# Routing by one table of pairwise comparisons, another order around the last tile, and block 2's list read first

## The chip, the cores and the metric

The kernel runs on one core of a Trainium2 chip. Each time is the device time of one execution in microseconds (us). The engines named below are PE (TensorE, the matrix multiplier), DVE (VectorE), ACT (ScalarE), POOL (GpSimd) and SP (SyncE, which here only starts DMAs). They run their own instruction streams and meet at semaphores.

## The reference

One step of a one-layer encoder over 1024 prompt frames and 32 sample frames, width 1024. First a mixer (an mLSTM with four heads and a multi-scale pooling), then a mixture of 16 experts in 4 groups of 4:

```python
x = x + mix @ w_out
x = x + hier_moe(rmsnorm(x, norm2_g), w_rg, b_rg, w_re, b_re, w_gate, w_up, w_down)

def hier_moe(x, ...):
    pg = softmax(x @ w_rg + b_rg)                 # 4 groups
    pg_top, g_idx = top_k(pg, 1)
    le = (x @ w_re + b_re) of the group chosen    # 4 experts
    pv, pi = top_k(softmax(le), 2)
    pv = pv / sum(pv)
    y = sum over the 2 experts e: pg_top * pv_e * ((silu(x @ w_gate[e]) * (x @ w_up[e])) @ w_down[e])
```

`top_k` takes the lower index where two values are equal.

## The kernel before

**Tiles.** The 1056 rows are nine tiles (`NT` = 9, `LAST` = 8) of 128 rows, the sample frames being a tile of 32. In a round `i` of a loop over the tiles every engine does its part of tile `i` (projections), tile `i-1` (mLSTM, pooling, `w_out`) and tile `i-2` (router). Each engine's order is the order in which the code is written. The block `if i == NT` is round 9: the rest of the last tile and the router of tile 7 (`LAST - 1`), without projections to fill PE. Round 10 holds the router of tile 8.

**Router of a tile.** PE transposes the tile (`h2_transposes`), DVE scales it into `h2T` (`h2_evac`, L1016), PE multiplies by the router weights (`router`), DVE copies (`partial_logits`, `lgT`, L1056), PE sums (`router_sums`), DVE adds the bias (`logits`, L1062). `routing` then finds the group and two experts in three calls of `first_max` (L1068 to L1072), 24 small DVE instructions that each wait for the one before. It writes one-hot rows `oh[:, t, 0..2, :]`, the third being the sum (L1096). PE counts with it (`ranks`), and DVE (`places`, L1136 to L1144) turns the counts into a slot for each row in its expert's list. POOL writes the entries into the lists in HBM (`scatter`, L541).

**Experts.** After the tiles come 16 blocks of at most 150 rows of one expert (150 rows in blocks 1 and 2, then six of 130, two of 135, two of 140, and 150 again). For a block POOL reads its list (`load_ids`, L557), gathers its rows from HBM in 5 indirect DMAs (L551), DVE transposes them (`gather_turn`, L1407) and scales them (`gather_scale`, L1413), PE does gate and up (`gate_up`, L1527) and down, ACT and DVE the silu and the product (`products`, L1428), DVE turns the results back (`results`, L1436) and weighs them (`gate_rows`, L1443), and POOL adds them into `z_d` in 5 indirect DMAs (L599). `results` of block j waits until the additions of block j-1 have landed. SP loads an expert's weights (3 MB) when PE has freed the former ones. Block 1 is put together early: the rows of tiles 0 to 6 that belong to it are gathered (`first`, turned by `first_turn`, L1115), those of tiles 7 and 8 are picked by a matmul with a 0/1 matrix (`first_picks`, DVE L1109), and `first_rows` (L1129) sums both.

**POOL behind the tiles.** After `scatter(8)` POOL reads the list of block 1 (start of expert 0's list), copies it (L639), reads the list of block 2, gathers block 2, and then waits for the table of blocks, which DVE computes meanwhile, to read the list of block 3. Small instructions on `pad` (`stand`, `carry_wait`, L595, L499) stand between them.

## Time and profile before

| | us |
|---|---|
| median of 3 runs | 939.91 (939.53 to 940.20) |
| span of the profiled execution, first to last instruction | 939.7 |
| PE busy | 880.8 (94% of the span) |
| DVE busy | 431.1 (46%) |
| POOL busy | 374.6 (40%) |
| ACT busy | 154.5 (16%) |

The profiled execution was recorded with its span alone; nothing is recorded of what lies around it. The median of the other runs is 0.2 us more than this span. Times in rows are from the start of the span. A busy share is a mean over stages with different limits: what an edit is worth is read where it stands. L numbers are lines of the kernel before. "bank" is PSUM; `win` and `wout` name SBUF areas that the expert stage uses again for its own buffers, and `h_d` in the rows is the HBM copy of the normed rows.

### The profile page before, as it was taken

The page shows a single profiled execution, that of the slowest core. Times are in us where ns is not written, and L with a number is a line of the kernel's source. Part 1 is how long each engine was busy: PE and PEld are TensorE (multiplying, and loading weights), DVE is VectorE, ACT ScalarE, POOL GpSimd, SP SyncE. Part 2 cuts the span into 40 slices and gives each one's busy share as a digit, 9 for nine tenths or more (in the row PEclk, how much of TensorE's full clock was granted, in tenths as well). Part 3 has the DMA queues.
Part 4 walks back from the last instruction along what each step waited for, and adds up shares of the span by engine and source line. Part 5 has one row for each costly group of instructions (what it writes and reads, how often), then busy time and mean ns, then how long its engine had stood idle before and what let it go on. Part 6 is the DMA issues. An engine that isn't in the chain of part 4 may idle for free.

```text
span 939.7 us, 16689 instructions
## 1 busy us (share of the span) xinstructions
PE 880.8 (94%) x6339; PEld 755.1 (80%) x6339; DVE 431.1 (46%) x1166; ACT 154.5 (16%) x456; POOL 374.6 (40%) x576
## 2 busy tenths in 40 slices
PE   5989999999999999999989799999999999999960
PEld 3974987869588695886945699999999999999920
DVE  3144474645646456463557843333333333333264
ACT  2031212121311213111131210000000000000071
POOL 4040031210302103021150258767767776777524
PEclk9989999999999999999999899999999999999985
DMA  9930203030110301003027389999999999999883
GB/s 328 280 151 1 68 1 80 12 79 1 28 52 1 79 1 34 25 1 57 1 62 291 71 294 299 327 352 335 360 346 333 327 322 326 315 319 314 248 305 115
DMA packets 90039, 163.15 MB, mean 174 GB/s; under 512 B 48887, under 2 KB 59027, under 8 KB 81770
## 3 DMA queue, kind: packets, MB, share of 16 engines
q1 hardware_dynamic: 70062, 136.43, 41.5%
q0 software_dynamic: 17728, 25.28, 11.2%
q8 instruction: 41, 0.67, 0.3%
q10 hardware_dynamic: 2188, 0.59, 0.3%
q14 instruction: 20, 0.16, 0.0%
HBM read 139.83 MB, written 25.87 MB: 176 GB/s over the span
## 4 chain that ended last, share of the span: by engine, by line
PE 51%; DMA 16%; issue 11%; POOL 11%; DVE 9%; ACT 1%; POOLq 1%; DVEq 0%; SPq 0%; ACTq 0%
PE bank L1527 48%; DMA z_d<-wout,win 12%; POOL z_d L599 7%; DVE wout L1443 2%; POOL wout L551 2%; PE bank L1532 1%; DVE wout L1436 1%; DVE win L1482 1%; DMA wout<-h_d,idt 1%; DMA h2T<-z_d 1%; DVE win L1407 1%; PE bank L1732 0%; DMA xbuf<-in_x_prompt 0%; POOL pad L595 0%; PE bank L1645 0%
## 5 line engine op out<-in xcount | busy, mean ns | idle before, releaser
L1527 PE MATMUL bank<-wout,win 128*128 128x150 f32 (+3 forms) x2048 | 246.3, 282 | 1.1 <-DVE wout L1129 1.1
L1527 PEld LDWEIGHTS bank<-wout,win 128*128 128x128 f32 x2048 | 244.7, 190 | 1.2 <-DVE wout L1129 1.2
L1527 PE MATMUL bank<-hT,win 128*128 128x128 f32 (+1 forms) x1536 | 182.9, 279 | 0.0
L1527 PEld LDWEIGHTS bank<-hT,win 128*128 128x128 f32 x1536 | 178.6, 192 | 1.5 <-issue 1.2
L1527 PE MATMUL bank<-win 128*128 128x130 f32 (+5 forms) x1024 | 137.3, 294 | 2.7 <-DVE win L1428 1.4
L599 POOL DMA_INDIRECT z_d<-wout,win x75 | 125.2, 1669 | 27.1 <-issue 26.8
L1527 PEld LDWEIGHTS bank<-win 128*128 128x128 f32 (+2 forms) x1024 | 125.5, 191 | 12.3 <-issue 10.3
L1527 PE MATMUL bank<-win,hT 128*128 128x260 f32 (+3 forms) x512 | 122.2, 417 | 3.0 <-DVE xbuf L1247 1.5
L1527 PE MATMUL bank<-wout,mixT 128*128 128x512 f32 (+1 forms) x384 | 116.8, 487 | 1.8 <-ACT mixT L845 1.7
L1527 PEld LDWEIGHTS bank<-win,hT 128*128 128x128 f32 (+1 forms) x512 | 77.1, 173 | 43.0 <-issue 34.1
L1436 DVE STREAM_TRANSPOSE wout<-bank 128x480 f32<-128x480 f32 (+1 forms) x45 | 25.1, 603 | 156.7 <-DMA z_d<-wout,win 155.2
L1527 PEld LDWEIGHTS bank<-wout,mixT 128*128 128x128 f32 (+1 forms) x384 | 50.8, 163 | 57.1 <-issue 54.4
L534 POOL TENSOR_SCALAR_AFFINE_SELECT dexp<-dexp 128x512 f32<-128x512 f32 (+1 forms) x9 | 5.4, 596 | 200.2 <-DVE dexp L1051 200.2
L551 POOL DMA_INDIRECT wout<-h_d,idt x75 | 73.8, 984 | 20.8 <-issue 20.5
L927 ACT ACTIVATE win<-bank 128x150 f32<-128x150 f32 (+3 forms) x64 | 18.1, 287 | 330.9 <-PE bank L1527 308.7
L512 POOL COPY ulast<-ubuf 128x60 f32<-128x60 f32 x7 | 3.9, 555 | 119.5 <-ACT ubuf L824 119.4
L1407 DVE STREAM_TRANSPOSE win<-wout 128x1280 f32<-128x1280 f32 x15 | 37.8, 2517 | 13.0 <-DMA wout<-h_d,idt 13.0
L1428 DVE TENSOR_TENSOR win<-bank,win 128x150 f32<-128x150 f32 (+3 forms) x64 | 17.7, 293 | 50.6 <-ACT win L927 50.6
L541 POOL DMA_INDIRECT ids_d<-ent,slots x18 | 18.4, 1021 | 49.2 <-DVE slots L1144 44.7
L595 POOL TENSOR_TENSOR pad<-pad 1x1 f32<-1x1 f32 x61 | 18.3, 301 | 26.0 <-DMA z_d<-wout,win 13.3
L1034 DVE RECIPROCAL sig<-sig 128x512 f32<-128x512 f32 x8 | 26.8, 3352 | 0.3
L1443 DVE TENSOR_TENSOR wout<-wout,win 128x1280 f32<-128x1280 f32 x15 | 22.5, 1497 | 7.4 <-POOL win L610 5.8
(308 smaller groups left out, 812.0 us busy)
## 6 DMA issues: line engine op xcount, KB each, us to landing
win<-in_w_gate SPq DMA_DIRECT2D x32, 1024.0 KB, 6.3
win<-in_w_up SPq DMA_DIRECT2D x32, 1024.0 KB, 9.2
win<-in_w_down SPq DMA_DIRECT2D x32, 1024.0 KB, 10.6
win<-in_w_in SPq DMA_DIRECT2D x4, 2048.0 KB, 20.1
xbuf<-in_x_prompt SPq DMA_DIRECT2D x8, 512.0 KB, 3.8
wout<-in_w_out SPq DMA_DIRECT2D x1, 4096.0 KB, 15.6
z_d<-xbuf SPq DMA_DIRECT2D x32, 128.0 KB
h_d<-xn SPq DMA_DIRECT2D x8, 512.0 KB, 2.7
```

Of the source, the lines that this page charges most:

```text
L541: g.indirect_dma_start(out=ids_d, out_offset=bass.IndirectOffsetOnAxis(ap=slots[0:R, n, t:t + 1].bitcast(U32), axis=0), in_=ent[0:R, n, t, ...
L551: g.indirect_dma_start(out=dst[:, c, :], out_offset=None, in_=h2_q, in_offset=bass.IndirectOffsetOnAxis(ap=idt[:, c:c + 1].bitcast(U32), a ...
L595: g.tensor_tensor(pad[:, c:c + 1], pad[:, 0:1], pad[:, 0:1], ALU.mult)
L599: g.indirect_dma_start(out=z_q, out_offset=bass.IndirectOffsetOnAxis(ap=idp[:, c:c + 1].bitcast(U32), axis=0), in_=yrow[:, c, :], in_offse ...
L927: a.activation(sgl[:, f % 2, 0:n], B[GB[f]][:, 0:n], ACT.Silu).then_inc(silu_ready, 1)
L1034: link(v.reciprocal(sig[0:R, b, :], sig[0:R, b, :]))
L1407: v.transpose(xgS.rearrange("p k a i -> p a k i"), xg.rearrange("p a (i k) -> p a k i", k=KD)).then_inc(xt_raw, 1)
L1428: v.tensor_tensor(hid[:, f, 0:n], B[GB[f]][:, n:2 * n], sgl[:, f % 2, 0:n], ALU.mult).then_inc(hid_ready, 1)
L1436: v.transpose(yrow[:, :, 32 * m0:32 * m1].rearrange("p a (m i) -> p m a i", i=32), y_window(b, m1 - m0, r)).then_inc(y_ready, 1)
L1443: v.tensor_tensor(yrow, yrow, ents[3][:, :, 1:2].broadcast_to([P, NP, PIECE]), ALU.mult).then_inc(y_gated, 1)
L1482: out = v.scalar_tensor_tensor(out=dq, in0=sq, scalar=fs[0:R, 3, c:c + 1], in1=wq, op0=ALU.mult, op1=ALU.mult)
L1527: return nc.tensor.matmul(out, lhsT, rhs, start=first, stop=last)
```

## The change

- `routing` compares all pairs of four values at once, for the group logits and the four groups of expert logits together (a 5 x 4 x 4 table `duel`), and sums it both ways to give each value its rank. The group is the one with the highest rank, the two experts those with the two highest. After 8 instructions `oh[:, t, 2, :]` is written and PE may count. The rest is split into `picks_of` (3 instructions), `gaps` (5) and `shares` (3). In rounds 2 to 8 they stand one behind the other where `routing` stood.
- Round 9 on DVE is in another order: `mix_start` of tile 8 (without its last instruction, now `decayed`) stands ahead of `norm_x1` of tile 7; `new_state` and `partial_logits(7)` stand behind the instruction that ACT waits for; `first_turn` is split into 2, 2 and 1 pieces. On ACT the copy `xp` of tile 7 (L855) stands behind the decay matrix of tile 8.
- The router of tile 8 stands in round 9, its slots (`seats`) behind `first_rows`; `seats(7)` behind `places(8)`; the scaling of the normed tile 8 (`scale_x1`) behind `gaps(8)`.
- On PE the state transposes stand behind `ranks(8)`, and the first half of tile 8's transposes need no longer wait for the second half of its residual.
- POOL reads block 2's list and gathers its rows first, then reads block 1's list, then block 3's.

```diff
@@ POOL
+            load_ids(CAP)
+            fetch_block(2, 1, 2)
             load_ids(0)
-            pool.wait_ge(ids_in, 32)
-            g.tensor_copy(ents[0], idraw).then_inc(carried, 1)
-            pool.wait_ge(carried, 2)
-            load_ids(CAP)
-            g.tensor_copy(ents[1], ents[0]).then_inc(rolled, 1)
-            pool.wait_ge(rolled, 1)
-            fetch_block(2, 2)
             after(pool, "table_ready", 1)
...
+            pool.wait_ge(ids_in, 48)
+            stand(4)
+            g.tensor_copy(ents[2], idraw).then_inc(rolled, 2)
+            pool.wait_ge(rolled, 2)
+            pool.wait_ge(carried, 4)
+            g.tensor_copy(ents[1], ents[0]).then_inc(carried, 2)
+            pool.wait_ge(carried, 6)
             load_ids(pool.value_load(tabi[0:1, NB + 3:NB + 4], min_val=0, max_val=NE * CAP))
-            pool.wait_ge(carried, 5)
-            g.tensor_copy(ents[2], ents[1]).then_inc(rolled, 1)
-            pool.wait_ge(rolled, 2)
-            g.tensor_copy(ents[1], ents[0]).then_inc(carried, 1)
-            pool.wait_ge(carried, 6)
             fetch_block(3, 6)
@@ ACT, round 9
                     decay_matrix(LAST)
+                    picked_rows(LAST - 1)
                     head_norm(LAST)
                     mix_a(LAST)
                     route_exps(LAST - 1)
                     norm_2(LAST)
+                    picked_rows(LAST)
@@ DVE
+                link(v.tensor_tensor(ge, five.unsqueeze(3).broadcast_to(cubed), five.unsqueeze(2).broadcast_to(cubed), ALU.is_ge))
+                link(v.tensor_tensor(ge, ge, below[0:R].unsqueeze(1).broadcast_to(cubed), ALU.mult))
+                link(v.tensor_reduce(out=ahead, in_=ge, axis=AX.X, op=ALU.add))
+                link(v.tensor_reduce(out=lost, in_=ge.rearrange("p g a b -> p g b a"), axis=AX.X, op=ALU.add))
+                link(v.tensor_tensor(rank, lost, ahead, ALU.subtract))
+                link(v.tensor_tensor(goh, rank[:, 0], seat[0:R, 0], ALU.is_equal))
+                two = cube_of(R)
+                link(v.tensor_tensor(two, rank[:, 1:], seat[0:R, 1].unsqueeze(1).broadcast_to([R, EG, EPG]), ALU.is_le))
+                v.tensor_tensor(oh[0:R, t, 2, :].rearrange("p (g e) -> p g e", e=EPG), two, wide(goh, [R, EG, EPG]), ALU.mult
+                                ).then_inc(S["route_ready"], 1)
@@ DVE, round 9
                     mix_start(LAST)
+                    norm_x1(LAST - 1)
+                    decayed(LAST)
                     mix_b(LAST)
                     h2_evac(LAST - 1)
-                    first_turn()
+                    first_turn(range(0, 2))
                     numerators(LAST)
-                    partial_logits(LAST - 1)
                     head_out(LAST)
                     logits(LAST - 1)
                     routing(LAST - 1)
+                    picks_of(LAST - 1)
+                    gaps(LAST - 1)
+                    first_turn(range(4, NP))
                     first_scale()
+                    shares(LAST - 1)
                     residual(LAST)
                     places(LAST - 1)
                     h2_evac(LAST)
-                    norm_x1(LAST)
-                    continue
+                    dve.wait_ge(pick_ready, 1)
+                    rms_x1(LAST)
+                    partial_logits(LAST)
+                    logits(LAST)
+                    routing(LAST)
+                    picks_of(LAST)
+                    places(LAST)
+                    seats(LAST - 1)
+                    gaps(LAST)
+                    scale_x1(LAST)
+                    first_rows()
+                    shares(LAST)
+                    seats(LAST)
+                    break
@@ DVE, in head_out
+                if t == LAST:
+                    new_state(LAST)
+                    partial_logits(LAST - 1)
+                    first_turn(range(2, 4))
                 after(dve, "hs0", t + 1)
@@ PE, round 10
                     first_picks(LAST - 1)
-                    state_transposes()
                 if 2 <= i:
                     ranks(i - 2)
                 if i == NT + 1:
+                    state_transposes()
                     first_picks(LAST)
```

The instructions of DVE and POOL in their order, at the three places that matter (a time is not in these rows).

**Place 1: DVE in round 9, from the norm of tile 7 to `h2_evac(7)`.** `sm` is the rms of tile 7 and `xn` its normed rows; PE's pooling matmul waits for `dcy`; `dexp` is the decay matrix. Before:

```order
L1259 TENSOR_SCALAR xn<-xbuf,sm 128x1024
L1041 COPY hmt<-bank 128x128
L1043 COPY dcy<-bank 128x4
L1046 TENSOR_TENSOR kw<-bank,hmt 128x512
L1051 TENSOR_TENSOR dexp<-bank,dexp 128x512
L1236 TENSOR_TENSOR mixT<-bank,psc 128x512
L1016 TENSOR_TENSOR h2T<-bank,g 128x512 x2
```

Now:

```order
L1048 COPY hmt<-bank 128x128
L1050 COPY dcy<-bank 128x4
L1053 TENSOR_TENSOR kw<-bank,hmt 128x512
L993 TENSOR_SCALAR sm<-sm 128x1
L994 TENSOR_TENSOR sm<-sm 128x1
L995 TENSOR_TENSOR sm<-sm 128x1
L996 TENSOR_SCALAR sm<-sm 128x1
L997 TENSOR_TENSOR sm<-sm 128x1
L1306 TENSOR_SCALAR xn<-xbuf,sm 128x1024
L1063 TENSOR_TENSOR dexp<-bank,dexp 128x512
L1276 TENSOR_TENSOR mixT<-bank,psc 128x512
L1023 TENSOR_TENSOR h2T<-bank,g 128x512 x2
```

The three instructions on `hmt`, `dcy` and `kw` moved ahead of the norm of tile 7; `dexp` stayed behind it.

**Place 2: DVE behind `places(8)`.** The first two rows are the pick of tile 8, `slotf` and `slots` the list places, the `wout` row is `first_rows`, `kw<-cnt` the start of the table. Before:

```order
L1107 SCALAR_TENSOR_TENSOR rt<-oh,rt 128x1
L1109 TENSOR_SCALAR win<-place_of,rt,sm 128x150
L1142 TENSOR_TENSOR rt<-oh,rt 128x16
L1143 TENSOR_REDUCE slotf<-rt 128x1
L1142 TENSOR_TENSOR rt<-oh,rt 128x16
L1143 TENSOR_REDUCE slotf<-rt 128x1
L1144 CAST slots<-slotf 128x2
L1129 SCALAR_TENSOR_TENSOR wout<-bank,g2m,win 128x5x30 x8
L1359 SCALAR_TENSOR_TENSOR kw<-cnt,iof 128x16
```

Now, behind the pick of tile 8 (`kept` holds the places of tile 7):

```order
L1174 TENSOR_TENSOR rt<-oh,kept 128x16
L1175 TENSOR_REDUCE slotf<-rt 128x1
L1174 TENSOR_TENSOR rt<-oh,kept 128x16
L1175 TENSOR_REDUCE slotf<-rt 128x1
L1176 CAST slots<-slotf 128x2
L1115 TENSOR_REDUCE rt<-rt 128x1
L1116 TENSOR_TENSOR rt<-rt 128x4
L1117 TENSOR_TENSOR rt<-oh 128x16
L1118 TENSOR_TENSOR rt<-rt 128x16
L1119 TENSOR_REDUCE rt<-rt 128x1
L1306 TENSOR_SCALAR xn<-xbuf,sm 128x1024
L1154 SCALAR_TENSOR_TENSOR wout<-bank,g2m,win 128x5x30 x8
```

and behind `first_rows`:

```order
L1124 SCALAR_TENSOR_TENSOR rt<-rt 128x1
L1126 RECIPROCAL ent<-rt 128x1
L1127 TENSOR_TENSOR ent<-ent,rt 128x1
L1174 TENSOR_TENSOR rt<-oh,rt 128x16
L1175 TENSOR_REDUCE slotf<-rt 128x1
L1174 TENSOR_TENSOR rt<-oh,rt 128x16
L1175 TENSOR_REDUCE slotf<-rt 128x1
L1176 CAST slots<-slotf 128x2
L1429 SCALAR_TENSOR_TENSOR kw<-cnt,iof 128x16
```

Between the pick of tile 8 and `first_rows` stand 11 instructions instead of 5, and tile 8's own slots stand behind `first_rows`, ahead of the table.

**Place 3: POOL behind the last scatter.** `idraw` receives a list, the `wout` rows are the 5 gathers of a block. Before:

```order
L557 DMA idraw<-ids_d 128x1x10 [waits h2_stored,out_done,scat1,scat0]
L639 COPY win<-idraw 128x10 [waits ids_in]
L557 DMA idraw<-ids_d 128x1x10 [waits carried]
L642 COPY win<-win 128x10
L595 TENSOR_TENSOR pad<-pad 1x1 [waits xt_raw,ids_in,rolled]
L562 TENSOR_SCALAR idt<-idraw,qf 128x5
L564 COPY win<-idraw 128x10
L499 TENSOR_TENSOR pad<-pad 1x1 [waits carried]
L551 DMA wout<-h_d,idt 128x256 x5
L646 TENSOR_LOAD tabi [waits table_ready]
L646 ISA x2
```

Now:

```order
L564 DMA idraw<-ids_d 128x1x10 [waits h2_stored,out_done,scat1,scat0]
L602 TENSOR_TENSOR pad<-pad 1x1 [waits xt_raw,ids_in]
L569 TENSOR_SCALAR idt<-idraw,qf 128x5
L571 COPY win<-idraw 128x10
L506 TENSOR_TENSOR pad<-pad 1x1 [waits carried]
L558 DMA wout<-h_d,idt 128x256 x5
L564 DMA idraw<-ids_d 128x1x10
L648 TENSOR_LOAD tabi [waits table_ready]
L648 ISA x2
```

and from there to block 3's list:

```order
L602 TENSOR_TENSOR pad<-pad 1x1 [waits ids_in]
L657 COPY win<-idraw 128x10
L660 COPY win<-win 128x10 [waits carried,rolled]
L662 TENSOR_LOAD tabi [waits carried]
L662 ISA x2
L564 ISA
L564 DMA idraw<-ids_d 128x1x10
L602 TENSOR_TENSOR pad<-pad 1x1 [waits xt_raw,ids_in]
L569 TENSOR_SCALAR idt<-idraw,qf 128x5
```

One list load instead of two stands ahead of block 2's gathers, and behind them block 1's list is awaited before block 3's is asked for.

## Rows read from the trace of the kernel before

**Rows 1.** The page: span, then each engine's busy time, share of the span, instructions.

```profile
span 939.7 us, 16689 instructions
...
PE 880.8 (94%) x6339; PEld 755.1 (80%) x6339; DVE 431.1 (46%) x1166; ACT 154.5 (16%) x456; POOL 374.6 (40%) x576
```

**Rows 2.** Timeline, PE, 461 to 551: start, busy us, work [idle before <- releaser].

```profile
461.92 0.29 PE L1527 MATMUL bank<-oh,ustrict 128*128 128x16 f32 x2
...
493.07 1.13 PE L1527 MATMUL bank<-dlt,poolw 128*128 128x128 f32 x8 [2.69 <-DVE dcy L1043]
...
508.35 0.66 PE L1732 MATMUL bank<-ident,isb 128*128 128x128 f32 x4 [1.18 <-DVE isb L1209]
...
520.67 0.65 PE L1527 MATMUL bank<-h2T,wr 128*32 128x128 f32 x16 [1.97 <-DVE h2T L1016]
...
522.93 4.35 PE L1527 MATMUL bank<-win 128*128 128x150 f32 x16
...
534.27 16.59 PE L1527 MATMUL bank<-wout,win 128*128 128x150 f32 x128 [1.15 <-DVE wout L1129]
```

**Rows 3.** Waits of PE, 560 to 900: us in total, times, longest.

```profile
PE bank L1527 <- DVE win L1428: 1.4, 3, 0.7
```

**Rows 4.** Timeline, DVE, results of blocks 3, 10, 11, 14 and 15.

```profile
608.06 1.65 DVE L1436 STREAM_TRANSPOSE wout<-bank 128x480 f32<-128x480 f32 x3 [8.16 <-DMA z_d<-wout,win]
...
766.34 1.65 DVE L1436 STREAM_TRANSPOSE wout<-bank 128x480 f32<-128x480 f32 x3 [14.33 <-DMA z_d<-wout,win]
...
789.60 1.64 DVE L1436 STREAM_TRANSPOSE wout<-bank 128x480 f32<-128x480 f32 x3 [14.70 <-DMA z_d<-wout,win]
...
856.67 1.65 DVE L1436 STREAM_TRANSPOSE wout<-bank 128x480 f32<-128x480 f32 x3 [9.50 <-DMA z_d<-wout,win]
...
875.49 0.68 DVE L1436 STREAM_TRANSPOSE wout<-bank 128x480 f32<-128x480 f32 x1 [3.81 <-DMA z_d<-wout,win]
```

**Rows 5.** Timeline, DVE, 452 to 538.

```profile
452.60 0.15 DVE L1068 TENSOR_REDUCE rt<-rt 128x1 f32<-128x4 f32 x1
...
457.16 0.18 DVE L1096 TENSOR_TENSOR oh<-oh 128x16 f32<-128x16 f32 x1
...
492.57 0.28 DVE L1041 COPY hmt<-bank 128x128 f32<-128x128 f32 x1
...
531.31 0.17 DVE L1144 CAST slots<-slotf 128x2 int32<-128x2 f32 x1
531.88 2.34 DVE L1129 SCALAR_TENSOR_TENSOR wout<-bank,g2m,win 128x150 f32<-128x150 f32 x8 [0.40 <-PE bank L1527]
...
537.28 0.29 DVE L1370 TENSOR_TENSOR kw<-kw,rt 128x128 f32<-128x128 f32 x1
```

**Rows 6.** Timeline, ACT, at 490.8.

```profile
490.81 2.04 ACT L855 ACTIVATE win<-xbuf 128x1024 f32<-128x1024 f32 x1
```

**Rows 7.** Window 522 to 523: us, PE busy, granted clock, DMA share, GB/s.

```profile
522.00:523.00 1.00, 0.51 (x3) 0.50 0.01 1
```

**Rows 8.** Timeline, POOL, 532 to 559.

```profile
532.28 0.96 POOL L541 DMA_INDIRECT ids_d<-ent,slots  x1 [9.93 <-DVE slots L1144]
...
536.76 0.76 POOL L557 DMA_DIRECT2D idraw<-ids_d  x1 [2.24 <-issue]
...
539.53 0.70 POOL L557 DMA_DIRECT2D idraw<-ids_d  x1 [0.30 <-POOL win L639]
...
549.09 0.79 POOL L557 DMA_DIRECT2D idraw<-ids_d  x1
...
555.93 1.39 POOL L595 TENSOR_TENSOR pad<-pad 1x1 f32<-1x1 f32 x1 [5.59 <-DVE win L1407]
...
558.19 1.09 POOL L551 DMA_INDIRECT wout<-h_d,idt  x1 [0.17 <-issue]
```

**Rows 9.** DMA issues of 549 to 550: KB each, median us to landing.

```profile
idraw<-ids_d POOLq DMA_DIRECT2D x1, 5.0 KB, 4.3
```

**Rows 10.** The same for 536 to 537.5.

```profile
idraw<-ids_d POOLq DMA_DIRECT2D x1, 5.0 KB, 2.2
```

More of the change, by code:

```diff
@@ L1098, in routing, with shares @@
+            def shares(t):
+                R = ROWS[t]
                 after(dve, "rexp", t + 1)
@@ L1319, in _ @@
                     routing(i - 2)
+                    picks_of(i - 2)
+                    gaps(i - 2)
+                    shares(i - 2)
                     places(i - 2)
```

114 lines of the change are left out of this document (69 added, 45 removed).

## The prediction

> **What bounds the kernel now.** I read the page first. PE is busy for 94% of the span and DVE, POOL and ACT for less than half of it [rows 1], so an edit on DVE pays only where PE, or what decides the end, waits for it. PE's timeline shows where that is. In the tile rounds PE comes to `ranks` at 461.92 without a wait, and DVE had the one-hot rows ready at 457.34; the waits stand behind 488, in rounds 9 and 10: 2.69 us for `dcy`, 1.18 for the heads, 1.97 for `h2T`, 1.15 for `first_rows` [rows 2, 5]. At 522 to 523 the granted clock is 0.50, the 1.2 GHz level, after two thirds of the time since 517.6 stood idle, and `first_picks(7)` takes 4.35 us there, twice the 2.2 that it takes at 2.4 GHz [rows 2, 7].
>
> Then the expert stage. PE looks full, but it waits three times for DVE's products, 1.4 us in all [rows 3]. DVE's `results` waits in every block for the landing of the block before (8.16, 14.33, 14.70, 9.50 us) [rows 4]. These landings form a second chain: landed additions, results, weighing, 5 scatter issues on POOL, landing. Between blocks 3 and 14 it takes (856.67 - 608.06)/11 = 22.6 us a block [rows 4]. PE takes less for the 130-row blocks and more for the 150-row blocks: the chain falls behind, stops PE where PE waits for products, and gets level again at block 15, where `results` waits 3.81 us for the landing and then still for PE. So the end moves by what the chain moves; what PE alone gains at its start is lost again in the three waits. I follow both.
>
> **The change part by part.**
>
> *Routing in the seven tile rounds.* 24 dependent instructions take 457.34 - 452.60 = 4.74 us [rows 5]. No trace shows the 80-wide compare. 16 elements cost 0.18 and 128 elements 0.29 [rows 5]; these are the bounds, and I take 0.24 from the line between them. Four such and four of about 0.17, with 0.035 between two, give 1.9 us up to `route_ready` (1.7 with the small price for all, 2.1 with the large one). In these rounds PE comes 4.6 us later than the result, so the cover is wide and I take 0 for them; the instructions put behind it (11, some 2.1 us) keep the sum below the old one.
>
> *Round 9, first half.* `dcy` is copied right after the residual. DVE copies `hmt` at 492.57 now [rows 5], behind ACT's three instructions and the norm; it can at 489.1, so PE starts pooling at 490.3 instead of 493.07. The next wait is for the decay product: ACT starts it behind a copy of 2.04 us that began at 490.81 [rows 6]; without it DVE's product ends 1.0 us earlier than before, POOL's mask follows, and PE idles 0.9 us. Since the long idle stretch goes, I let PE keep 2.4 GHz there. I get the router of tile 7 at 496.0 against 499.3: 3.3 us. `head_out` then no longer stands behind `new_state` and `lgT` (four and one instructions, 1.05 us): the heads reach PE at 504.0 instead of 508.35, 4.35 us earlier. This holds through `w_out`, since DVE's longer list there ends at 510.7 and the second half of the residual comes at 512.5.
>
> *Round 9, second half.* `seats(7)`, five instructions of 0.2 with their gap, leaves the way: 0.95. The scaling of the normed tile leaves it: 0.75. So the logits of tile 8 come 6.05 us earlier, 6.3 if the clock holds; the routing gives 2.8 less than 4.7: `route_ready` at 518.95 instead of 527.8. `first_picks(7)` ends then too if it runs at 2.4 GHz. Counts and state transposes change places, the pick of tile 8 is ready at 520.65, 9.9 us earlier. But DVE now does 11 instructions (0.95 + 0.95 + 0.75 us) ahead of `first_rows`: that starts at 523.25 instead of 531.88 and PE begins block 1 at 525.6 instead of 534.27 [rows 2, 5], 8.65 us earlier. This is PE's lead, not yet the end's.
>
> *Slots of tile 8.* They are cast at 531.31 (ready 531.48) [rows 5], ahead of `first_rows`. Now `first_rows` (2.34), `shares` (0.55) and `seats` (0.95) come first: 527.1, only 4.4 us earlier. Queued behind them on DVE is the table; it ends near 537, and its readers come later than that. On POOL everything waits for these slots.
>
> *POOL's list loads.* From the first list load to the second it is 539.53 - 536.76 = 2.77 us [rows 8]. This trip leaves the way to block 2's gathers: 4.4 + 2.8 = 7.2 us, so the last gather, which ended at 549.09, ends at 541.9. What is late next is block 3. Before, its list was asked for at 549.09 and lay ready when `stand` could go at 555.93 [rows 8]. Now block 1's list goes first: asked for at 541.9, landed 4.3 later [rows 9] at 546.2, two copies with their gaps 0.9, a register load and the issue about 1.0; then block 3's own load, asked for at 548.1. Its landing is bounded by 2.2 (quiet queue) [rows 10] and 4.3 [rows 9]; I take the middle, since the gathers are gone from the queue but weights are under way. So the list is in at 551.3, while DVE turned block 2 at 548.6 already: a new wait of 2.7 us. `stand`, 1.39 us long beside DVE's scaling [rows 8], should fall behind it and be short; 1.1 us later the gathers of block 3 begin, 552.4 instead of 558.19 [rows 8]. The chain starts 5.8 us earlier. Ends: 2.2 and 0.4 for load and issue give 7.4; both trips at 4.3 and a long `stand` give 3.5.
>
> The Trainium skill, "DMA: Bandwidth & Descriptors", section on the anatomy of one DMA, gives a fixed cost of about 2.0 us to such a small load, whatever it stands behind. Rows 9 and 10 differ by twice with the same 5 KB. By that rule both trips would cost 2.0, the list would lie there when block 2 is turned, and the sum would be about 1.5 us lower; the row of 4.3, from this very place, decides.
>
> *What the lead does to the chain.* PE's lead over the chain grows by 8.65 - 5.8 = 2.85 us. The late blocks, where the lag is large, have longer steps (block 10 to 11: 789.60 - 766.34 = 23.26 [rows 4]). If the first three or four steps take 0.3 more each for the earlier lag, 1.0 us is lost. Bounds: 0, and 0.66 in each of 12 steps (below).
>
> Sum: 939.7 - 5.8 + 1.0 = 934.9 for this execution; its span is 0.2 under the median, so 935.1.
>
> **The rivals.**
>
> *The clock still falls in round 10.* For: PE still idles 1.5 and 0.5 us around 514 to 516.5, and it fell after such idling before [rows 7]. Against: half of that idling is gone. Then `first_picks(7)` costs 4.35, not 2.2, counts and pick come 2 us later, and slots and chain with them: 937.0.
>
> *PE leads, the chain follows.* If the landings are long only because the DMA engines are behind, an earlier start of the weights moves them too, or block 3's list comes in unnoticed. Then the end moves 8.3 us: 931.6. Against: `results` waits for landings in every block already.
>
> *Nothing reaches the end.* The lists take the long end (3.5), the clock falls (2.0) and the chain gives 1.0 back: 939.4.
>
> *Slower, by the chain's step.* One mechanism: with the weights of each block asked for earlier against the scatters, landings take longer in every step, not only the first. At the longest step seen, 23.26 against 22.6, 12 steps cost 7.9 us: 939.9 - 5.8 + 7.9 = 942.0. It decides from 0.48 us a step on. For: the long steps are those with the largest lag. Against: late steps with large lag were as often normal, and PE's waits would cap the lag as they do now.
>
> **How the numbers follow.** 935.1 has 0.45, the clock 0.25, PE's lead 0.15, nothing 0.09, slower 0.06. The likeliest case alone reaches from 933.5 to 937.5. The range that leaves out 2 in 10 takes in PE's lead and the clock case with its long trips: 931.3 to 938.6. A measurement here tells 0.2%, 1.9 us, from no change. Under 938.0 lie the first and third cases and nearly all of the clock case: 0.84; within 0.2%: 0.10; slower: 0.06.
>
> **What will show it.** Right: pooling of tile 8 on PE without a wait near 490.3; heads at 504; PE's first expert matmul at 525 to 526 and the last `slots` cast near 527; gathers of block 2 beginning near 535.8; a wait of POOL for block 3's list of 2 to 3 us, and its gathers near 552; PE's waits for products growing from 1.4 to about 4 us; `results(3)` near 602. Wrong: a clock of 0.50 around 518 (then 937), block 3's gathers before 550 (then under 934), steps over 23 us on average (then no gain), or a PE that shows no more waits than before while the end still moves by over 8 us.

## The result, and the profile after

The changed kernel takes 942.77 us (median of 14 runs, 940.44 to 945.47), the kernel before 940.07 (14 runs): ratio 1.0033, 95% interval 1.0023 to 1.0043. It is slower by a third of a per cent; the forecast was 935.1. Timed once more it gave 1.0026 (1.0016 to 1.0037). The two profiled executions of the changed kernel have spans of 939.8 and 940.6, the two of before 939.7 and 936.7; a span is 1.6 to 2.0 below its run's time. Both profiles of the change are needed, since they lose the gain in two places. Left out of the rows and ratios below are one run of e3, 2601.6 us long, and one of the kernel before, 1880.1 us.

The page of the first (the same parts as in [rows 1]):

```profile
span 939.8 us, 16630 instructions
...
PE 876.3 (93%) x6339; PEld 751.2 (80%) x6339; DVE 427.0 (45%) x1106; ACT 154.6 (16%) x456; POOL 371.5 (40%) x575
```

PE's timeline, first profile of the change (columns as in [rows 2]; L1597 answers to L1527 there):

```profile
488.23 1.06 PE L1597 MATMUL bank<-dlt,poolw 128*128 128x128 f32 x8
...
519.42 2.28 PE L1597 MATMUL bank<-win 128*128 128x150 f32 x16 [0.21 <-DVE win L1134]
...
523.89 2.31 PE L1597 MATMUL bank<-wout,win 128*128 128x150 f32 x16 [1.15 <-DVE wout L1154]
...
557.05 18.39 PE L1597 MATMUL bank<-wout,win 128*128 128x150 f32 x128 [8.39 <-DVE wout L1483]
...
583.47 14.45 PE L1597 MATMUL bank<-wout,win 128*128 128x130 f32 x128
```

Rounds 9 and 10 went as forecast: no wait for `dcy`, and PE starts the experts at 523.89, in the second profile at 524.38, where it started at 534.27 [rows 2] and in the second profile of before at 532.57. Then it waits 8.39 us ahead of block 2, and block 3 starts at 583.47, with the kernel before at 583.39. The second profile loses it elsewhere, a part ahead of block 2 and 5.28 us inside it:

```profile
524.38 1.95 PE L1597 MATMUL bank<-wout,win 128*128 128x150 f32 x11 [1.15 <-DVE wout L1154]
...
552.45 16.59 PE L1597 MATMUL bank<-wout,win 128*128 128x150 f32 x128 [1.62 <-DVE wout L1483]
574.31 11.33 PE L1597 MATMUL bank<-win 128*128 128x150 f32 x64 [5.28 <-issue]
585.48 6.75 PE L1597 MATMUL bank<-wout,win 128*128 128x130 f32 x59
```

In both profiles PE waits for nothing from block 3 to the last block, so the gain is gone when block 3 starts. The reason stands on POOL. First profile (answers to [rows 8]; L548 scatters list entries, L564 loads a list, L558 gathers rows; the small `pad` at L602 starts when the list is in):

```profile
522.01 0.98 POOL L548 DMA_INDIRECT ids_d<-ent,slots  x1 [0.30 <-issue]
528.84 0.97 POOL L548 DMA_INDIRECT ids_d<-ent,slots  x1 [5.84 <-DMA ids_d<-ent,slots]
...
533.09 0.77 POOL L564 DMA_DIRECT2D idraw<-ids_d  x1 [2.01 <-issue]
540.05 0.18 POOL L602 TENSOR_TENSOR pad<-pad 1x1 f32<-1x1 f32 x1 [6.19 <-DMA idraw<-ids_d]
...
541.14 1.11 POOL L558 DMA_INDIRECT wout<-h_d,idt  x1 [0.17 <-issue]
...
547.27 0.78 POOL L564 DMA_DIRECT2D idraw<-ids_d  x1
553.80 0.18 POOL L602 TENSOR_TENSOR pad<-pad 1x1 f32<-1x1 f32 x1 [5.75 <-DMA idraw<-ids_d]
...
555.71 0.70 POOL L564 DMA_DIRECT2D idraw<-ids_d  x1 [1.27 <-DVE win L1477]
557.98 0.18 POOL L602 TENSOR_TENSOR pad<-pad 1x1 f32<-1x1 f32 x1 [1.57 <-DMA idraw<-ids_d]
...
559.04 1.11 POOL L558 DMA_INDIRECT wout<-h_d,idt  x1 [0.18 <-issue]
```

The second profile of the change, the same stretch:

```profile
533.72 0.77 POOL L564 DMA_DIRECT2D idraw<-ids_d  x1 [2.11 <-issue]
536.00 0.18 POOL L602 TENSOR_TENSOR pad<-pad 1x1 f32<-1x1 f32 x1 [1.52 <-DMA idraw<-ids_d]
...
543.20 0.78 POOL L564 DMA_DIRECT2D idraw<-ids_d  x1
549.90 0.18 POOL L602 TENSOR_TENSOR pad<-pad 1x1 f32<-1x1 f32 x1 [5.92 <-DMA idraw<-ids_d]
...
551.80 0.70 POOL L564 DMA_DIRECT2D idraw<-ids_d  x1 [1.27 <-DVE win L1477]
558.22 0.18 POOL L602 TENSOR_TENSOR pad<-pad 1x1 f32<-1x1 f32 x1 [5.71 <-DMA idraw<-ids_d]
...
559.28 1.11 POOL L558 DMA_INDIRECT wout<-h_d,idt  x1 [0.18 <-issue]
```

Read the pairs of load and `pad`: the same 5 KB take 7.0, 6.5 and 2.3 us in the first profile and 2.3, 6.7 and 6.4 in the second. Together the three take 15.8 and 15.4 us, and block 3's rows are asked for at 559.04 and 559.28, behind the 558.19 of [rows 8], where the forecast had 552.4.

What stands beside them is SP's queue of the first profile, block 2's weights (with the kernel before, the first of them is issued at 542.79):

```profile
532.41 0.35 SPq L380 DMA_DIRECT2D win<-in_w_gate  x1
532.80 0.43 SPq L380 DMA_DIRECT2D win<-in_w_up  x1
540.51 0.33 SPq L380 DMA_DIRECT2D win<-in_w_gate  x1
540.88 0.44 SPq L380 DMA_DIRECT2D win<-in_w_up  x1
544.60 4.47 SPq L386 DMA_DIRECT2D win<-in_w_down  x2
```

and the windows (us, busy time of each engine, clock, DMA share, GB/s), first before, then the change:

```profile
533.00:540.00 7.00, 5.85 (x48) 5.76 (x47) 6.35 (x23) 0.00 (x0) 2.63 (x5) 1.00 0.07 8
```

```profile
533.00:540.00 7.00, 7.00 (x57) 7.00 (x56) 2.57 (x12) 2.06 (x4) 0.77 (x1) 1.00 0.89 303
547.00:554.00 7.00, 1.67 (x14) 1.44 (x12) 1.01 (x1) 0.00 (x0) 1.24 (x4) 1.00 1.01 371
556.00:558.00 2.00, 0.95 (x4) 0.95 (x5) 2.00 (x3) 0.00 (x0) 0.43 (x2) 0.50 0.09 3
```

A list takes 7.0 and 6.5 us where the DMA share is 0.89 and 1.01, and 2.3 us where it is 0.09; before it found 0.07. SP asks for block 2's weights when PE is through the first half of block 1's gate and up, 8.5 us behind PE's start of block 1 both before (534.27, 542.79) and in the first profile (523.89, 532.41), so PE's gain brought them here.

In the second profile SP asks 10.2 us behind that start, since PE's granted clock fell to 0.50, the 1.2 GHz level, in the middle of it. That profile's first weights, and the window 526 to 528 of the first and the second profile:

```profile
534.58 0.35 SPq L380 DMA_DIRECT2D win<-in_w_gate  x1
526.00:528.00 2.00, 2.00 (x18) 2.00 (x17) 1.83 (x6) 0.00 (x0) 0.00 (x0) 1.00 0.12 26
526.00:528.00 2.00, 2.00 (x10) 2.00 (x9) 1.77 (x6) 0.00 (x0) 0.00 (x0) 0.50 0.31 75
```

Block 1 takes PE 26.4 us there, without its wait, and 24.8 in the first profile. With the 8.5 us of the first profile the weights would have been asked for at 532.9 (an estimate), 0.8 us ahead of the list at 533.72: by this estimate it is the slower clock that let this list through, at a price of 1.7 us in block 1.

Inside block 2 of the second profile, DVE explains the wait that has no named releaser on PE:

```profile
566.52 1.55 DVE L1513 TENSOR_TENSOR wout<-wout,win 128x1280 f32<-128x1280 f32 x1 [12.58 <-POOL win L617]
571.32 2.48 DVE L1477 STREAM_TRANSPOSE win<-wout 128x1280 f32<-128x1280 f32 x1 [3.24 <-DMA wout<-h_d,idt]
573.72 0.49 DVE L1498 TENSOR_TENSOR win<-bank,win 128x150 f32<-128x150 f32 x2
```

Block 2's products (573.72), which PE needs, stand behind the turn of block 3's rows, and these have landed only at 571.3.

### The profile page after: what moved, and what is told of

The parts are those of the page before. It is cut to its first block and busy times, and to the rows that moved or that the text cites. A ratio compares the mean times of both kernels' runs of the same rounds, so it can differ in the third digit from the quotient of the medians.

```text
span 939.8 us, 16630 instructions
## 1 busy us (share of the span) xinstructions
PE 876.3 (93%) x6339; PEld 751.2 (80%) x6339; DVE 427.0 (45%) x1106; ACT 154.6 (16%) x456; POOL 371.5 (40%) x575
## 5 line engine op out<-in xcount | busy, mean ns | idle before, releaser
L1597 PE MATMUL bank<-wout,win 128*128 128x150 f32 (+3 forms) x2048 | 248.2, 283 | 9.5 <-DVE wout L1483 8.4
L1597 PEld LDWEIGHTS bank<-wout,win 128*128 128x128 f32 x2048 | 246.5, 191 | 9.8 <-DVE wout L1483 8.6
L1597 PE MATMUL bank<-hT,win 128*128 128x128 f32 (+1 forms) x1536 | 182.9, 279 | 0.0
L1597 PEld LDWEIGHTS bank<-hT,win 128*128 128x128 f32 x1536 | 178.6, 192 | 1.5 <-issue 1.2
L1597 PE MATMUL bank<-win 128*128 128x130 f32 (+5 forms) x1024 | 135.0, 291 | 0.3 <-DVE win L1134 0.2
L1597 PEld LDWEIGHTS bank<-win 128*128 128x128 f32 (+2 forms) x1024 | 123.5, 188 | 9.8 <-issue 9.4
L1597 PE MATMUL bank<-win,hT 128*128 128x260 f32 (+3 forms) x512 | 121.1, 415 | 3.3 <-DMA win<-in_w_in 1.8
L1597 PE MATMUL bank<-wout,mixT 128*128 128x512 f32 (+1 forms) x384 | 116.8, 487 | 1.7 <-ACT mixT L849 1.7
L1597 PEld LDWEIGHTS bank<-win,hT 128*128 128x128 f32 (+1 forms) x512 | 76.5, 172 | 42.7 <-issue 33.5
L1597 PEld LDWEIGHTS bank<-wout,mixT 128*128 128x128 f32 (+1 forms) x384 | 50.8, 163 | 57.1 <-issue 54.4
L558 POOL DMA_INDIRECT wout<-h_d,idt x75 | 74.6, 994 | 20.8 <-issue 20.8
L548 POOL DMA_INDIRECT ids_d<-ent,slots x18 | 18.3, 1018 | 49.5 <-DVE slots L1176 39.2
L602 POOL TENSOR_TENSOR pad<-pad 1x1 f32<-1x1 f32 x62 | 17.9, 289 | 27.7 <-DMA idraw<-ids_d 13.5
```

The lines of the kernel that those rows point to most:

```text
L548: g.indirect_dma_start(out=ids_d, out_offset=bass.IndirectOffsetOnAxis(ap=slots[0:R, n, t:t + 1].bitcast(U32), axis=0), in_=ent[0:R, n, t, ...
L558: g.indirect_dma_start(out=dst[:, c, :], out_offset=None, in_=h2_q, in_offset=bass.IndirectOffsetOnAxis(ap=idt[:, c:c + 1].bitcast(U32), a ...
L602: g.tensor_tensor(pad[:, c:c + 1], pad[:, 0:1], pad[:, 0:1], ALU.mult)
L1597: return nc.tensor.matmul(out, lhsT, rhs, start=first, stop=last)
```

## The experiments

Five rounds each, ratio to the kernel before run beside it on the same chip; each group of runs (e, f, g, h, i) had another chip. "Rows 3" is POOL's first gather for block 3, "PE 3" PE's start of block 3, "last" the end of PE's last expert work, all of one profile (us).

| kernel | rows 3 | PE 3 | last | span | median | ratio (95%) |
|---|---|---|---|---|---|---|
| before | 558.19 | 583.39 | 908.15 | 939.7 | 940.1 | |
| before, again | 556.51 | 581.69 | 904.29 | 936.7 | 939.6 | 0.9994 (0.9983, 1.0006) |
| changed | 559.04 | 583.47 | 906.48 | 939.8 | 942.8 | 1.0033 (1.0023, 1.0043) |
| changed, again | 559.28 | 585.48 | 908.08 | 940.6 | 942.3 | 1.0026 (1.0016, 1.0037) |
| e1 weights after list | 559.05 | 583.02 | 906.79 | 938.7 | 940.4 | 1.0009 (0.9993, 1.0025) |
| e2 changed, old lists | 561.00 | 587.78 | 910.38 | 943.9 | 946.5 | 1.0072 (1.0057, 1.0087) |
| e3 before, new lists | 560.79 | 582.72 | 908.81 | 941.0 | 941.8 | 1.0024 (1.0008, 1.0040) |
| e4 scatters together | 553.25 | 576.19 | 899.59 | 931.8 | 936.5 | 0.9959 (0.9943, 0.9974) |
| f1 own list buffer | 560.26 | 586.79 | 909.76 | 944.4 | 945.4 | 1.0018 (0.9985, 1.0050) |
| f2 e3 and own buffer | 556.53 | 583.27 | 906.49 | 940.9 | 941.2 | 1.0008 (0.9998, 1.0019) |
| f3 both mends | 548.95 | 574.06 | 896.67 | 931.9 | 932.8 | 0.9912 (0.9892, 0.9932) |
| f3, again | 549.13 | 574.43 | 898.01 | 933.4 | 934.8 | 0.9953 (0.9936, 0.9969) |
| f7 weights after rows | 548.85 | 575.85 | 898.45 | 933.7 | 934.5 | 0.9930 (0.9909, 0.9950) |
| g1 routing alone | 557.29 | 582.64 | 905.25 | 938.0 | 939.7 | 0.9998 (0.9988, 1.0008) |
| g2 no ACT stores | 554.39 | 579.16 | 901.76 | 934.0 | 938.8 | 0.9996 (0.9978, 1.0014) |
| h1 products first | 558.77 | 584.76 | 908.68 | 942.3 | 943.7 | 1.0045 (1.0028, 1.0063) |
| h3 f3, slots first | 550.98 | 577.51 | 900.11 | 934.6 | 936.2 | 0.9964 (0.9952, 0.9977) |
| h5 f3, products first | 549.66 | 574.89 | 897.49 | 932.8 | 934.0 | 0.9949 (0.9931, 0.9967) |
| i1 e1, products first | 559.56 | 581.43 | 906.74 | 939.0 | 941.1 | 1.0014 (0.9997, 1.0031) |
| i2 e1, again | 560.21 | 583.30 | 906.87 | 939.3 | 940.8 | 1.0009 (0.9992, 1.0025) |

Over all twenty profiles "last" comes 346.3 to 350.0 us behind "rows 3" and 322.6 to 326.1 behind "PE 3"; in nine of them PE runs the last stretch in 322.6 without a wait. The ratio isn't that of the medians: f1 has two of its twelve runs near 934.7, and its ratio is 1.0018 where the medians alone would give 1.0054.

**e1, block 2's weights after its list.** In the changed kernel:

```
+                sp.wait_ge(ids_in, 32)
                 load_gate_up(1, half)
```

> The changed kernel, with block 2's gate and up weights asked for on SP only once block 2's list has landed. Theory (the list's load collides with these weights: it is asked for at 533.09, 0.7 us after them, and takes 6 to 7 us where it took 2.2): the list lands in 2.2 to 3 us, the first gather of block 2 is issued near 536.5 instead of 541.14, gathers of block 3 near 554 instead of 559.04, PE's wait ahead of block 2 shrinks from 8.4 to about 4 us, and the end is 4 to 5 us under the changed kernel (about 938.3, ratio to before 0.998). Rival (the list is slow whatever the weights do, POOL being late through its scatters alone): landing stays at 6 us or more, the weights only come later, end the same as the changed kernel or 1 to 3 us over it.

The list lands in 2.3 us and the first gather is issued at 537.29: the weights made it slow. But block 1's list, asked for at 543.40 between the weights of 542.97 and 546.61, takes 6.9 us, and block 3's, asked for at 552.22, 5.8. Block 3's rows are no earlier than in the changed kernel. The theory is right on the collision and wrong on its worth: it only moves to the next list. The time did fall by about 2 us against the changed kernel, here and in i2 (1.0009 twice, against 1.0033 and 1.0026), where 4 to 5 had been expected; rows 3, PE 3 and "last" don't show where these 2 us come from.

**e2 and e3, the order of the lists by itself.** e2 puts POOL's old sequence (block 1's list, copy, block 2's list, gathers, block 3's list) into the changed kernel, e3 the new one (`load_ids(CAP)`, `fetch_block(2, 1, 2)`, `load_ids(0)`, copies, block 3's list) into the kernel before.

> The changed kernel with POOL's lists in the order of before (block 1's list first, then block 2's), all else as changed. Theory (the new order is worth its trip, the collision is the fault): two trips of which the first takes 6 to 7 us; block 2's first gather near 545 instead of 541.1, the end 1 to 4 us over the changed kernel (944 to 947). Rival (the new order is the fault, since block 1's list now stands in the way of block 3's): gathers of block 3 come at or before 558, the end under the changed kernel by 1 to 3 us.

> The kernel before with POOL's lists alone in the new order. Theory (without PE's lead the weights of block 2 are asked for at 542.8, behind the list's landing): landing 2.2, block 2's first gather near 540.2 instead of 542.96, gathers of block 3 1 to 2.5 us earlier than 558.19, end 1 to 2.5 us under before (937.6 to 939). Rival (the order is the fault): block 3's list comes late, its gathers at or behind 558.2, the end the same as before or up to 3 us over it.

e2: as the theory, 4 us over the changed kernel; PE waits 9.2 us ahead of block 2. e3: the rival. POOL in e3:

```profile
539.98 1.11 POOL L551 DMA_INDIRECT wout<-h_d,idt  x1 [0.18 <-issue]
...
546.09 0.79 POOL L557 DMA_DIRECT2D idraw<-ids_d  x1
551.73 0.18 POOL L595 TENSOR_TENSOR pad<-pad 1x1 f32<-1x1 f32 x1 [4.85 <-DMA idraw<-ids_d]
...
553.63 0.70 POOL L557 DMA_DIRECT2D idraw<-ids_d  x1 [1.27 <-issue]
559.73 0.18 POOL L595 TENSOR_TENSOR pad<-pad 1x1 f32<-1x1 f32 x1 [5.40 <-DMA idraw<-ids_d]
...
560.79 1.11 POOL L551 DMA_INDIRECT wout<-h_d,idt  x1 [0.18 <-issue]
```

Block 2's gathers come 3.0 us earlier than before (542.96), block 3's 2.6 later than in [rows 8]: two lists one behind the other now stand between them, 5.6 and 6.1 us, where block 3's alone was asked for at 549.09 and was hidden. The order saves a trip where it doesn't count and puts one where it does, without any lead of PE.

**e4, g2, the scatters.** e4: POOL issues tile 8's entries without waiting for tile 7's.

```
+                if t == LAST - 1:
+                    return
                 for name in ("scat0", "scat1"):
                     after(pool, name, 16 * (t + 1))
```

g2 leaves out ACT's eight stores of the recurrent state, normalisers and pooling history, so it doesn't return these outputs.

> The changed kernel, in which POOL doesn't wait for the landing of tile 7's scattered list entries before it issues tile 8's (it waits for both behind them). Theory (collision): scatters of tile 8 at 525.4 instead of 528.84, the list asked for near 530, ahead of the weights at 532.4, and landed in 2.2 to 3 us; block 2's first gather near 534 instead of 541.1; the end 5 us or more under the changed kernel (936 to 938.5). Rival (the landing of a list is slow for another reason, not by what is asked beside it): the list is asked for 3.3 us earlier and still takes 6 us or more, gathers near 538, end 2 to 3 us under the changed kernel.

> The changed kernel without ACT's eight stores of the recurrent state, normaliser, pooling history (these outputs are left out), which are issued from 520.98 to 525.8. Theory S (POOL's scatter of tile 7's entries, issued at 520.5 and 522.0, takes 5.8 us to land since these stores, in lines of a few bytes, stand in the queues beside it): landing in 2 to 2.5 us, tile 8's scatter at 525.5 instead of 528.84, the list asked for near 529.5, ahead of the weights at 532.4, and the end as with the scatters together, 5 to 7 us under the changed kernel (936 to 938). Rival (it's SP's 512 KB store of the normed rows at 521.62, which stays): scatter of tile 8 at 528 to 529 as before, end the same as the changed kernel.

e4 does what the theory says: scatter at 526.91, list asked for at 531.46, ahead of the weights (533.72), in after 2.3 us, block 3's rows at 553.25, 5.8 us ahead of the changed kernel. g2: the wait for tile 7's entries falls from 5.8 to 3.7 us, not to 2. SP's 512 KB store stays and may be the rest; no run takes it away. In its profile the list then lands in 2.3 us and block 3's rows are asked for at 554.39. Its runs spread from 935.6 to 945.1; the ratio lies under that of the changed kernel (0.9996 against 1.0026, intervals apart) and shows no gain over before. That the stores share in the hold-up is shown; its worth is read better from e4, which leaves nothing out.

**f1, f2, f3, a tile of its own for block 1's list,** so that block 3's is asked for straight behind the gathers; f3 adds e4 and asks for block 1's right behind block 2's:

```
             load_ids(CAP)
+            load_ids(0, idone, idone_in)
             fetch_block(2, 1)
...
+            load_ids(pool.value_load(tabi[0:1, NB + 3:NB + 4], ...))
+            pool.wait_ge(idone_in, 16)
+            g.tensor_copy(ents[2], idone).then_inc(rolled, 2)
```

> The changed kernel, with block 1's list landing in a tile and on a semaphore of its own, so that block 3's list is asked for right behind block 2's gathers instead of behind block 1's list and two copies. Theory A (block 3's list stands on the chain: block 1's list takes 6 to 7 us beside block 2's weights, and only then is block 3's asked for, another 2 to 6 us): POOL waits for DVE's turn of block 2 and no list, block 3's gathers come at 556 to 557 instead of 559.0, and as block 2's are as late as in the changed kernel (541), the end is 2 to 3 us under the changed kernel (939.5 to 941). Rival B (what counts is only the landing of block 2's gathers, 552.99 with the changed kernel, and the lists are hidden): no difference from the changed kernel, 942 to 943.5.

> The kernel before with the new list order and block 1's list in a tile of its own. Theory A: with the list order alone block 2's gathers came 3.0 us earlier but block 3's 2.6 us later, since block 3's list was asked for at 553.6 and took 6 us; with its own buffer block 3's gathers come at 555 to 556 instead of 560.8, and the end is 938 to 939, 1.5 to 2.5 us under before and 3 to 4 under the order alone. Rival B (the order alone is slow because the gathers meet something else): 942 as with the order alone.

> The changed kernel with both mends on POOL: tile 7's and tile 8's list entries scattered without a wait between them, and block 1's list in a tile of its own, asked for right behind block 2's. Theory A: block 2's list and block 1's land before the weights of block 2 are under way (asked for at 533.7), first gather of block 2 near 535.5, block 3's list asked for near 542 and landed before block 2 is turned at 546.5, block 3's gathers near 549.5 instead of 553.25 with the scatters alone; end 2 to 3.5 us under the scatters alone (933 to 934.5). Rival B (block 3's gathers 3.7 us earlier are given back, PE being the bound, or later landings): same as with the scatters alone, 936 to 937.

f1 is a miss: the list of block 2 is as late as ever (6.9 us), its rows land at 555.33, PE waits 9.1 us ahead of block 2. Its runs lie at 940 to 948.6 with two of twelve at 934.6 and 934.8; neither of these two has a profile. f2: block 3's rows 4.3 us earlier than in e3, as expected, but no gain over before (1.0008); why 1.7 us less than [rows 8] buys nothing is open, the second profile of before had 556.51 as well. f3 is as expected; POOL in f3:

```profile
531.06 0.76 POOL L568 DMA_DIRECT2D idraw<-ids_d  x1 [2.15 <-DMA ids_d<-ent,slots]
531.83 0.70 POOL L568 DMA_DIRECT2D idone<-ids_d  x1
533.32 0.18 POOL L606 TENSOR_TENSOR pad<-pad 1x1 f32<-1x1 f32 x1 [0.79 <-DMA idraw<-ids_d]
...
540.80 0.77 POOL L568 DMA_DIRECT2D idraw<-ids_d  x1
...
546.68 1.40 POOL L606 TENSOR_TENSOR pad<-pad 1x1 f32<-1x1 f32 x1 [4.46 <-DVE win L1481]
...
548.95 1.09 POOL L562 DMA_INDIRECT wout<-h_d,idt  x1 [0.17 <-issue]
```

No list is waited for on the way to block 3, PE runs blocks 1 to 3 without a wait, and the change with both mends is 0.5 to 0.9% under before. PE starts block 3 7.3 to 9.3 us earlier than in the two profiles of before. How much the mends would give without the change is known for the list order with the buffer (f2, 1.0008); the scatters weren't tried there. A second timing:

> The kernel with both mends on POOL once more, for a firm ratio and a second profile: 932 to 934, ratio to before 0.991 to 0.993; PE starts block 3 near 574 without a wait behind block 1's start, 322.6 us later its last expert work ends.

Its ratio is 0.9953, at 934.8 us. The two intervals don't meet (they rest on five and six runs), so the gain is told as that range.

**f7, weights only after block 2's rows have landed** (SP waits for `gathered`, on top of f3).

> As the kernel with both mends on POOL, and block 2's gate and up weights asked for only once block 2's gathered rows have landed. Theory C (the weights are what makes gathers and lists slow: 5.5 to 6.1 us from the last issue to landing beside them, 2.9 to 4.1 without): gathers land in 2 to 3 us, near 544, block 3's gathers near 548; but the weights, asked for near 544, need 7 us a half, so PE waits 1 to 3 us ahead of and in block 2 and the end is 0 to 2 us over the kernel with both mends. Rival (the weights don't matter to the gathers): gathers land as in the kernel with both mends, PE waits more, end 3 us or more over it.

Rows land at 543.91, in f3 at 543.99: once the lists are ahead of the weights, there is nothing left to win for the rows. PE starts block 3 1.8 us later, but not by the weights: it waits for nothing from block 1 to block 3 in either. In f7 the granted clock is 0.50 at 526 to 528, in f3 1.00, and block 1 takes 26.3 us instead of 24.6. So the rival is right on the landing, its longer wait of PE did not come, and f7 gives no price for the delay.

**g1, the new routing alone in the kernel before.**

> The kernel before with the new routing alone (one table of comparisons), its picks, gaps and shares right behind it, everything else in the place it had. Theory P (the end follows PE's start of block 3 one for one, as nine profiles so far show 322.6 to 324.8 us from there to PE's last expert work, apart from one of 326.1): the routing of tile 8 is ready 2.8 us earlier, PE's first expert matmul comes near 531.5 to 532.5 instead of 534.27, block 2's rows (landed at 553.2 before, wanted by PE at 558.9) don't stand in its way, and the end is 1.5 to 2.5 us under before (938 to 939). Rival (routing is covered everywhere): same as before.

A miss. PE starts the experts at 533.52, between the two profiles of before (534.27 and 532.57), where 531.5 to 532.5 was expected. DVE needs 6.85 us from tile 8's logits to its slots, 7.24 in the second profile of before: the result is earlier, but picks, gaps and shares stand right behind it. By itself, then, the table shows no gain; the new order with the old routing wasn't tried.

**Once more, before and changed.**

> The kernel before once more, for a second profile: PE's block 1, 2 and 3 start without a wait 24.6 and 24.5 us apart, near 534, 558.7 and 583.2, and its time is 940.4 as the median so far; the first profile (span 939.7) was at the slow end of the runs, so this one's span should be 938 to 939 and the difference should show between PE's last expert work and the end, or in PE's waits of 560 to 900.

> The changed kernel once more, for a second profile: PE starts block 1 at 523.9 to 525.5, waits 8 to 9.2 us ahead of block 2 for its rows, block 3 at 583.5 to 587. If the first profile was a lucky one among its runs (939.8 against a median of 941), this one has block 3 nearer to 585 and the time near 942.8. Theory P then gives the end from block 3's start.

**h1, h5, i1, i2, block 2's products ahead of the turn of block 3's rows on DVE.**

```
+            products(2, r2)
             gather_turn(2)
-            products(2, r2)
```

> The changed kernel, with DVE making block 2's products before it turns block 3's rows (for block 2 alone; the blocks behind it keep their order). Theory D (in the changed kernel's second profile DVE waits for the landing of block 3's rows until 571.32, block 2's products stand behind that turn, and PE waits 5.3 us for them ahead of block 2's second matmuls): PE's wait there falls from 5.3 to 1 us or less, since block 1's rows are weighed from 566.5 to 568.1 and the products come right behind; block 3 starts near 581 instead of 585.5 (or, when block 2's list was late and PE waited 8.4 us ahead of block 2, near 583 as before, no gain), and the end is 2 to 4 us under the changed kernel (938.5 to 940.5). Rival (PE's wait comes from something else, its releaser being unknown to the profile): 942 to 943, wait unchanged.

> Both mends on POOL and block 2's products ahead of the turn of block 3's rows. With the mends DVE turns block 3's rows at 557.9, ahead of the products anyway, so Theory D expects no difference from the kernel with both mends (932 to 934); a gain of 2 us or more would mean that the turn still holds PE.

> The changed kernel with both block 2's weights held back until its list has landed and, on DVE, block 2's products ahead of the turn of block 3's rows. With the weights held back alone the list was in time and PE waited 3.6 us inside block 2 (573.11), DVE having turned block 3's rows from 570.12 on. Theory D (block 2's products stand behind that turn): products follow the weighing, which ends at 567.9; PE's second matmuls of block 2 start without a wait near 569.6, block 3 near 578 to 579.5 instead of 583.0, end 3 to 5 us under the kernel with the weights held back alone (936 to 937.5). Rival (what PE waits for is something else, or the gain is given back by the later turn): wait unchanged, or the end within 1 us of that kernel.

> The changed kernel with block 2's weights held back until its list has landed, once more beside the run above: 940.4, list landed in 2.3 us, PE's wait of 3 to 5 us ahead of block 2's second matmuls while DVE waits for block 3's rows, block 3 near 583.

h1 met a late list of block 2 (6.8 us, PE waits 9.3 us ahead of block 2) and tells nothing on the wait inside it; it is slower than before, as the changed kernel. h5: no difference from f3, as expected. PE in i1:

```profile
555.14 18.26 PE L1605 MATMUL bank<-wout,win 128*128 128x150 f32 x128 [4.59 <-DVE wout L1484]
573.24 8.35 PE L1605 MATMUL bank<-win 128*128 128x150 f32 x64
581.43 10.77 PE L1605 MATMUL bank<-wout,win 128*128 128x130 f32 x95
```

The wait inside block 2 (1.67 us in i2, 3.6 in e1) is gone, so the turn made it. But PE waits 2.2 us for products later, "last" is the same to 0.13 us and so is the time: a PE that is 1.9 us earlier gains nothing while block 3's rows stay at 559.6. That is the chain of the prediction at work.

**h3, tile 8's weights and slots ahead of the first block's rows, on top of f3.**

> Both mends on POOL, and DVE makes tile 8's weights and slots before the first block's rows instead of behind them. The slots are ready 2 us earlier (524.7 instead of 526.6), block 2's first gather comes near 533, but PE's first expert matmul is 1.5 us later (eight instructions and the wait for ACT's exponentials stand ahead of the rows): 526.5. Theory P (PE's start of block 3 sets the end, and both lists and rows are in time already): end 1 to 1.5 us over the kernel with both mends. Rival (POOL's chain still sets the end): 1.5 to 2 us under it.

936.2, 1.4 to 3.4 us over f3. The slots are earlier, but tile 8's entries are now scattered at 523.69, beside the stores, and POOL waits 4.6 us for them, so block 2's first gather comes only 0.5 us earlier (534.15). Rows and PE are both later (2.0 and 3.5 us), so it doesn't tell the two limits apart; 2.6 of PE's 3.5 are block 1 itself, with a granted clock of 0.50 at 526 to 530.

## Why the prediction was wrong

*What bounds the kernel: half right.* The forecast had one chain, POOL's, with PE following. i1, e3 and the table bear the chain out. But there are two limits of nearly the same length: in the second profile of before, in both of the changed kernel and in f3 PE waits for nothing behind block 3. PE's waits for products, which were to grow from 1.4 to about 4 us, were none in both profiles of the change. Both limits stood at or behind their old place in the changed kernel, 559.0 and 559.3 against 558.2 and 556.5 for the rows, 583.5 and 585.5 against 583.4 and 581.7 for PE.

*Routing, round 9, round 10: right; the clock: right in one profile of two.* The compare over 80 elements took 0.24 us, the strided reduce 0.29. Pooling started without a wait at 488.23 (forecast 490.3), the heads were at 502.02 (504.0), `route_ready` near 517.4 (518.95), PE's experts at 523.89 (525.6). The offset of 1.5 to 2.1 us is there ahead of round 9 already: PE begins the last tile's first transpose at 486.29 instead of 488.27. It belongs to the execution and not to the change, since the second profile of before has this transpose at 485.47. Counted from it, PE's experts start 8.4 us earlier in the first profiles and 8.5 in the second (46.0 and 47.1 us behind it before, 37.6 and 38.6 now), where the forecast had 8.65. `first_picks(7)` took 2.29 us, in the second profile 3.47, and `first_picks(8)` 2.28 in both: there the rival on the clock cost 1.2 us. It came back in block 1, with 1.7 us more, in that profile; the granted clock at 526 to 528 is 0.50 there and in e1, e2, f7, g2 and h3, and 1.00 in the first. That was no term of the forecast. Two slips of the text: the old routing has 23 dependent instructions, not 24, and DVE's decay product gains about 1.7 us, beside the offset, and not 1.0. A third: a span of the kernel before is 2.0 under its own run's time, so the profiled execution took about 941.7 us, and the "0.2 under the median" set a long execution against the middle of the others.

*Slots: right,* cast at 525.15, ready at 525.3 (forecast 527.1).

*POOL: the step that failed,* in three terms. First, a wait left out: `scatter` waits for its own landing, and tile 7's entries, which used to be long down when tile 8's were ready, now land beside ACT's eight stores, which were issued between 529 and 532 before and are issued between 521 and 525 now (DMA share 0.97 to 1.24 from 522 to 525). SP's 512 KB store of the normed rows did not move (521.62, before 522.26), and beside SP's stores alone the later of the two scatters landed in 3.1 us before; now it takes 6.1 in both profiles, and 3.9 in g2, without ACT's stores. That holds tile 8's scatter until 528.84, 2.7 us more than the 0.8 behind its slots of before. Second, block 2's list: 7.0 us instead of the 2.3 of before. With slots 1.8 earlier and the scatters' own trip 0.2 shorter: -1.8 + 2.7 - 0.2 + 4.7 = 5.4, and the first gather is at 541.14 instead of 535.8. Third, the trip of block 1's list: 547.27 to 555.71 is 8.4 us where the forecast had 6.2 (landing 6.5, not 4.3). The last list was short that time, 1.0 less than forecast: 552.4 + 5.4 + 2.2 - 1.0 = 559.0. In the second profile the first gather is only 1.3 late, the trip 2.4 longer and the last list's 3.2 longer: 552.4 + 6.9 = 559.3.

The forecast bounded block 3's list by 2.2 and 4.3 us, from a stretch in which weights had not yet been asked for or one whose load was counted to the gathers [rows 9, 10]: the list of 4.3 us was asked for at 549.09, where the DMA share is already 0.92 (547 to 554). It took the weights as given where they were. Its own second term, PE 8.65 us earlier, moves them by as much, into the very place of the lists. The bound had to come from a small load in the middle of a weight load, and the rival "slower, by the chain's step" looked for the collision in each block (the steps were not longer: results of block 3 at 608.73 and of block 14 at 849.10, 21.9 us each, was 22.6, and the row of block 14 names no landing any more) rather than at the start.

The Trainium skill's rule weighed there, a fixed cost of about 2.0 us for a small load ("DMA: Bandwidth & Descriptors", the anatomy of one DMA), agrees with the rows where little else moves (2.3 us at a DMA share of 0.09) and not with those beside a weight load (7.0 us at 0.89).

*The end.* From "last" to the end it takes 33.3 and 32.5 us in the changed kernel, 31.5 and 32.4 in before, and 34.5 to 35.4 in f3 and its kin. The tail reloads the sums behind block 15; its fifth load took 10.2 and 11.1 us to land with the kernel before, 11.9 and 11.2 with the changed one and 11.8 in f3. So f3 is 6.3 to 11.5 us ahead at "last" and 3.3 to 7.8 at the end. What makes the tail longer wasn't tried.

## What to carry to other kernels

When an engine on the path gets earlier, list the transfers that its progress releases, and place them on the new time axis beside every small load that something waits for; a landing read from a quiet stretch bounds nothing there. Ask for small lists before the big transfers of the same moment, into a buffer of their own, and don't let one small landing wait for another: in f3 that, with the scatters together, turned 1.003 into 0.991 to 0.995. And a reorder that takes one trip from the next consumer's way has to be followed to the consumer after it: in e3 block 2 gained 3.0 us and block 3 lost 2.6, and the kernel with it.

## What the runs showed of the hardware

A 5 KB load takes 2.2 to 2.4 us on idle DMA engines and 4.3 to 7.4 beside 1 MB weight loads; 3.1 to 3.7 in e2, e4 and g2, where it was asked for 0.5 to 1.2 us ahead of a pair of them. Which of the lists is hit turns on less than 1 us: 532.41 for the weights against 533.09 for block 2's list in one profile of the changed kernel (7.0 us), 534.58 against 533.72 in the other (2.3 us). The later of two scatters of 128 short entries took 6.1 us to land beside ACT's stores and SP's, 3.9 without ACT's, and 2.4 with neither (tile 8's, issued at 530.11 in the first profile of the change).

PE's granted clock fell to 0.50 within block 1 (526 to 528) in six of the fifteen profiles with the new order, and held at 1.00 in the others. Block 1 then took 26.3 to 27.2 us instead of 24.6 to 24.8. What decides between the two was not tried; in all of them PE had stood idle for part of 522 to 525.
